# First loads of a two-layer decoder step: order of use, half slabs, and four pieces of the second token half

## The chip, the core and the metric

The kernel runs as one launch on one core of one Trainium2 chip. The core has five engines with a queue of instructions each: TensorE (PE, matrix products), VectorE (DVE), ScalarE (ACT), GpSimd (POOL) and SyncE (SP, which here only issues transfers). Engines meet at semaphores. The metric is the device time of a launch in microseconds; lower is better.

## The reference, cut to what matters

Two layers work on 544 tokens (512 of a prompt, 32 new ones of eight running samples), each token 1024 numbers wide. Layer 0 mixes by a gated recurrence, layer 1 by attention in a sliding window; each is followed by a wide squared-ReLU network, and every residual is normalised. The change touches only the start of layer 0's mixer:

```python
y = jax.nn.gelu(x @ w_y + b_y, approximate=True)
u = x @ w_x + b_x
upad = jnp.concatenate([conv_buf.astype(u.dtype), u], axis=1)
xc = conv_b + sum(conv_w[k] * upad[:, k:k + T] for k in range(CONV_W))
r  = jax.nn.sigmoid(jnp.einsum('btni,nij->btnj', xb, w_ga) + b_ga)    # xb: xc in 8 blocks
gi = jax.nn.sigmoid(jnp.einsum('btni,nij->btnj', xb, w_gi) + b_gi)
a = jnp.exp(-LRU_C * r * jax.nn.softplus(-lam))
h[t] = a[t] * h[t-1] + mult[t] * gi[t] * xc[t]                        # as an associative scan
out = (h * y) @ w_out + b_out
```

## The kernel before, in words

**Layout.** Features lie on the 128 partitions, in eight tiles (k tiles); tokens lie along the free axis, in two halves: half 0 has prompt tokens 0 to 255, half 1 the other 256 and the 32 new ones (288 columns). Every product is made of three: each factor is split into a high part (a float32r copy, made by ACT) and a low part (what the copy lost, made by DVE), and hi·hi, lo·hi and hi·lo are added in PSUM. A split weight needs one ACT and one DVE instruction a slab (128 x 1024), a split pair of token tiles the same.

**Slabs.** SP loads weights in slabs of 512 KB into `stage`, which has four places. ACT's `split` waits for the arrival and writes `w_hi`; DVE's `split` writes `w_lo`, which also frees the place in `stage` (`slab_lo_done`). For pairs of output tiles, `w_x` and `w_y` come as two slabs each, of four k tiles by 256 columns.

**Order of the start.** SP issues, with no wait: tokens of half 0 in four pieces of two k tiles (256 KB each), with the first two slabs of `w_x` among them, the two slabs of `w_y`, then half 1 (1024 KB from `xp_t`, 128 KB from `xs_t` in runs of 32 numbers), and the gate weights once a place is free. ACT issues the vectors of biases and tables (213 KB) behind its first copy. ACT and DVE split the pieces in the order x, slab, x, x, slab, x, slab, slab. PE fills the start with 13 products of constants (`WARM`), then takes the first two `w_x` units k tile by k tile over both units (`group_by_k`), and the two `w_y` units whole, each once both slabs are split.

**The loop over s = 0 to 7** (four pairs of output tiles by two halves) follows. PE takes in step s two units of `w_x`, the gates of step s-1 and two units of `w_y`. ACT copies the `w_x` units to `u`; DVE runs the width-4 convolution into `xc`; ACT and POOL split `xc` (`xc_hi`, `xc_lo`); PE multiplies it by the gates; ACT takes tanh, exp and square root; DVE runs the recurrence (`recur`) and splits the next slabs. Before step 0's convolution, DVE does `derive_in` and `derive_series` (small steps toward a softplus of `lam`) and splits half 1 (`x_split(1)`); behind it comes `derive`. POOL scales the tokens for the residual (`residual0`) once the vectors have landed.

Each engine's order is that of the code. All that the change touches is in `build`: the SP block (lines 483 to 570), the heads of the ACT, DVE and PE blocks, and two inputs of `kernel`.

## Time and profile before

| what | value |
|---|---|
| median of three runs | 1097.09 us (1097.07 to 1097.62) |
| the profiled execution's own time | 1098.72 us |
| its span in the trace | 1096.9 us |
| PE busy | 1076.7 us (98%) |
| DVE, ACT, POOL busy | 802.6, 562.0, 163.7 us |
| granted TensorE clock, mean | 0.996 |

The span runs from the first to the last instruction; 1.82 us of the execution's time lie outside it. A time "at 16.91" is counted from the start of the span. A matmul's shown duration is longer than its step to the next one, because they are pipelined; the step is what a unit costs.

### The profile page before, as it was taken

The numbers are of one execution on the slowest core, as the hardware profiler recorded it, in microseconds if no ns is written. First come the engines' busy times: TensorE is split into PE (matmuls) and PEld (weight loads), VectorE is DVE, ScalarE is ACT, GpSimd is POOL, SyncE is SP. The second block draws the span as 40 slices with busy tenths as digits, with TensorE's granted clock in tenths as the row PEclk, the third lists the DMA queues.
The fourth block names the chain that finished last, engine by engine and source line by source line (L and its number), as shares of the span: only waits on it lengthen the run. The fifth ranks groups of instructions, "written<-read, shape, count | busy, mean of one in ns | idle before, by whom it ended". The sixth has DMA issues, their size and how long they took to land.

```text
span 1096.9 us, 22319 instructions
## 1 busy us (share of the span) xinstructions
PE 1076.7 (98%) x8535; PEld 1054.7 (96%) x8535; DVE 802.6 (73%) x1264; ACT 562.0 (51%) x995; POOL 163.7 (15%) x200
## 2 busy tenths in 40 slices
PE   8999999999999999999999999999999999999996
PEld 7999999999999999999999878999999999999996
DVE  6999899896758568566874574789958668586666
ACT  5999857652433425333666775665533424235233
POOL 2343042000000000011243564300000000000023
PEclk9999999999999999999999999999999999999998
DMA  7323224031413314173041221130423403234202
GB/s 248 115 87 97 74 63 136 19 116 58 136 40 133 117 36 134 44 245 101 20 135 45 61 59 38 48 108 1 154 65 110 134 24 129 72 101 135 77 1 82
DMA packets 63709, 98.66 MB, mean 90 GB/s; under 512 B 4384, under 2 KB 44768, under 8 KB 63616
## 3 DMA queue, kind: packets, MB, share of 16 engines
q1 hardware_dynamic: 62944, 94.81, 27.4%
q0 software_dynamic: 400, 2.21, 0.5%
q8 instruction: 51, 0.84, 0.3%
q10 hardware_dynamic: 288, 0.59, 0.2%
q14 instruction: 26, 0.21, 0.1%
HBM read 95.06 MB, written 3.56 MB: 90 GB/s over the span
## 4 chain that ended last, share of the span: by engine, by line
PE 80%; DVE 10%; ACT 4%; issue 2%; DMA 1%; POOL 1%; SPq 0%; DVEq 0%; ACTq 0%; POOLq 0%
PE bank L1921 10%; PE bank L1922 9%; PE bank L1923 9%; PE bank L2166 8%; PE bank L2168 8%; PE bank L2167 8%; PE bank L2140 6%; PE bank L2142 6%; PE bank L2141 6%; PE bank L1999 2%; PE bank L2001 2%; PE bank L2000 2%; DVE w_lo L1107 2%; PE bank L2275 1%; PE bank L2300 1%
## 5 line engine op out<-in xcount | busy, mean ns | idle before, releaser
L1114 DVE TENSOR_TENSOR w_lo<-stage,w_hi 128x1024 fp32r<-128x1024 f32 x120 | 144.8, 1219 | 56.1 <-ACT w_hi L648 56.1
L648 ACT ACTIVATE w_hi<-stage 128x1024 fp32r<-128x1024 f32 x120 | 124.4, 1054 | 112.5 <-DVE stage L1132 64.7
L1921 PE MATMUL bank<-x_hi,w_hi 128*128 128x288 f32 (+1 forms) x560 | 163.9, 293 | 1.4 <-issue 0.6
L1922 PE MATMUL bank<-m_lo,w_hi 128*128 128x288 f32 (+1 forms) x560 | 162.2, 290 | 0.0
L1922 PE MATMUL bank<-x_lo,w_hi 128*128 128x288 f32 (+1 forms) x560 | 161.7, 289 | 0.0
L1921 PE MATMUL bank<-m_hi,w_hi 128*128 128x288 f32 (+1 forms) x560 | 161.6, 289 | 0.0
L1923 PE MATMUL bank<-m_hi,w_lo 128*128 128x288 f32 (+1 forms) x560 | 161.6, 289 | 0.0
L1923 PE MATMUL bank<-x_hi,w_lo 128*128 128x288 f32 (+1 forms) x560 | 160.9, 287 | 0.0
L2140 PE MATMUL bank<-m_hi,w_hi 128*128 128x288 f32 (+1 forms) x512 | 147.7, 289 | 0.3 <-DVE m_lo L1457 0.3
L2142 PE MATMUL bank<-m_hi,w_lo 128*128 128x288 f32 (+1 forms) x512 | 147.6, 288 | 0.0
L2141 PE MATMUL bank<-m_lo,w_hi 128*128 128x288 f32 (+1 forms) x512 | 147.4, 288 | 0.0
L1469 DVE TENSOR_TENSOR acc<-bank,acc 128x288 f32<-128x288 f32 (+1 forms) x196 | 79.3, 436 | 69.0 <-PE bank L1923 56.2
L869 ACT ACTIVATE h<-bank 128x256 f32<-128x256 f32 (+1 forms) x72 | 28.1, 391 | 177.1 <-PE bank L2168 177.1
L2166 PE MATMUL bank<-s_hi,w_hi 128*128 128x288 f32 (+1 forms) x384 | 112.4, 293 | 0.0
L2167 PE MATMUL bank<-s_lo,w_hi 128*128 128x288 f32 (+1 forms) x384 | 112.1, 292 | 0.0
L2168 PE MATMUL bank<-s_hi,w_lo 128*128 128x288 f32 (+1 forms) x384 | 111.8, 291 | 0.0
L1921 PEld LDWEIGHTS bank<-x_hi,w_hi 128*128 128x128 f32 x560 | 105.2, 188 | 3.3 <-issue 2.4
L1921 PEld LDWEIGHTS bank<-m_hi,w_hi 128*128 128x128 f32 x560 | 105.7, 189 | 0.0
L1922 PEld LDWEIGHTS bank<-m_lo,w_hi 128*128 128x128 f32 x560 | 105.5, 188 | 0.0
L1922 PEld LDWEIGHTS bank<-x_lo,w_hi 128*128 128x128 f32 x560 | 105.3, 188 | 0.1
L1923 PEld LDWEIGHTS bank<-x_hi,w_lo 128*128 128x128 f32 x560 | 105.4, 188 | 0.0
L1923 PEld LDWEIGHTS bank<-m_hi,w_lo 128*128 128x128 f32 x560 | 105.3, 188 | 0.0
(271 smaller groups left out, 2792.4 us busy)
## 6 DMA issues: line engine op xcount, KB each, us to landing
stage<-w_up SPq DMA_DIRECT2D x64, 512.0 KB, 4.4
stage<-w_down SPq DMA_DIRECT2D x64, 512.0 KB, 3.7
stage<-w_qkv SPq DMA_DIRECT2D x10, 512.0 KB, 4.0
stage<-w_x SPq DMA_DIRECT2D x8, 512.0 KB, 5.2
stage<-w_y SPq DMA_DIRECT2D x8, 512.0 KB, 3.6
stage<-w_out SPq DMA_DIRECT2D x8, 512.0 KB, 3.7
stage<-w_o SPq DMA_DIRECT2D x8, 512.0 KB, 3.8
y_t<-acc SPq DMA_DIRECT2D x4, 288.0 KB, 2.4
```

Of the source, the lines that this page charges most:

```text
L648: A(hi, raw, ACT.Copy).then_inc(s_whi, 1)
L1114: vt.tensor_tensor(lo, raw, hi.bitcast(F32), ALU.subtract).then_inc(s_wlo, 1)
L1469: vt.tensor_tensor(a, bank[:, n0 % BANKS, :n], a, ALU.add).then_inc(s_evV, 1)
L1921: mm(out, wh, xh, start=(k == 0), stop=False)
L1922: mm(out, wh, xl, start=False, stop=False)
L1923: ins = mm(out, wl, xh, start=False, stop=(k == last))
L2140: mm(out, wh, xh, start=(k == 0), stop=False)
L2141: mm(out, wh, xl, start=False, stop=False)
L2142: ins = mm(out, wl, xh, start=False, stop=(k == 3))
L2166: mm(out, wh, xh, start=(fresh and k == 0), stop=False, skip_group_check=True)
L2167: mm(out, wh, xl, start=False, stop=False, skip_group_check=True)
L2168: ins = mm(out, wl, xh, start=False, stop=(k == 3), skip_group_check=True)
```

## The change

SP now issues the first loads in the order in which they are used, with the two `w_x` slabs in halves of 256 KB, and with a wait ahead of each from the fifth on: four pieces are out at a time. The two `w_y` slabs wait for the third and fourth token piece, and half 1 waits for the last half of `w_x`. Half 1 is one array now (`x_b`, 288 columns), loaded in four pieces of 288 KB with a semaphore each; half 0 is an array of its own too (`x_a`). ACT and DVE split x, half slab, x, half slab; the issue of the vectors moves behind ACT's third copy. DVE's `derive_series` moves from ahead of `x_split(1)` to behind the convolution and the gates' split. PE takes the `w_y` units of step 0 and the `w_x` units of step 1 by k tile too, and `WARM` is 11.

```diff
@@ -71,12 +71,12 @@
 PROBS = 3
 SPAN = 260
 STAGES = 4
-WARM = 13
+WARM = 11
 SLOTS = 8
 BANKS = 8
 
 
-def build(nc, xp_t, xs_t, vec, w_y, w_x, w_ga, w_gi, w_out, w_qkv, w_o, w_up, w_down,
+def build(nc, x_a, x_b, vec, w_y, w_x, w_ga, w_gi, w_out, w_qkv, w_o, w_up, w_down,
           ck_t, cache_k, cache_v, y_t, small, k_p, v_p, k_s, v_s):
     ctx = ExitStack()
     with ctx:
@@ -180,7 +180,9 @@
 
         s_vec = sem("vec_loaded")
         s_xa = [sem(f"x_half_a_loaded_{k}") for k in range(4)]
-        s_xb = sem("x_half_b_loaded")
+        s_xb = [sem(f"x_half_b_loaded_{k}") for k in range(4)]
+        s_early = [sem(f"first_half_of_slab_{k}_arrived") for k in range(2)]
+        s_halfhi, s_halflo = sem("half_slab_hi_done"), sem("half_slab_lo_done")
         s_arrived = [sem(f"slab_arrived_{i}") for i in range(STAGES)]
         s_whi, s_wlo = sem("slab_hi_done"), sem("slab_lo_done")
         s_unit = sem("unit_done")
@@ -540,23 +542,42 @@
 
             def load_x(k):
                 sp.dma_start(acc[:, 2 * k:2 * k + 2, 0:256],
-                             xp_t[256 * k:256 * k + 256, 0:256].rearrange("(k p) t -> p k t", p=128))\
+                             x_a[256 * k:256 * k + 256, :].rearrange("(k p) t -> p k t", p=128))\
                     .then_inc(s_xa[k], 16)
 
+            def load_half(j, part):
+
+                st = where[j][0]
+                k0 = 4 * j + 2 * part
+                sp.dma_start(stage[:, st, 512 * part:512 * part + 512].rearrange("p (k c) -> p k c", k=2),
+                             xv[:, k0:k0 + 2, 0:256]).then_inc(s_arrived[st] if part else s_early[j], 16)
+
+            def load_xb(k):
+                sp.dma_start(acc[:, 2 * k:2 * k + 2, 256:TOK],
+                             x_b[256 * k:256 * k + 256, :].rearrange("(k p) t -> p k t", p=128))\
+                    .then_inc(s_xb[k], 16)
 
             load_x(0)
-            load(0, xv[:, 0:4, 0:256])
-            for k in (1, 2):
-                load_x(k)
-            load(1, xv[:, 4:8, 0:256])
+            load_half(0, 0)
+            load_x(1)
+            load_half(0, 1)
+            sp.wait_ge(s_xa[0], 16)
+            load_x(2)
+            sp.wait_ge(s_early[0], 16)
+            load_half(1, 0)
+            sp.wait_ge(s_xa[1], 16)
             load_x(3)
-            load_pair(("pair", 0), yv, 0, 2)
+            sp.wait_ge(s_arrived[where[0][0]], 16)
+            load_half(1, 1)
+            sp.wait_ge(s_xa[2], 16)
+            load(2, yv[:, 0:4, 0:256])
+            sp.wait_ge(s_xa[3], 16)
+            load(3, yv[:, 4:8, 0:256])
+            sp.wait_ge(s_arrived[where[1][0]], 16)
+            for k in range(4):
+                load_xb(k)
             for p in range(4):
-                if p == 0:
-                    sp.dma_start(acc[:, :, 256:512],
-                                 xp_t[:, 256:512].rearrange("(k p) t -> p k t", p=128)).then_inc(s_xb, 16)
-                    sp.dma_start(acc[:, :, 512:TOK], xs_t.rearrange("(k p) t -> p k t", p=128)).then_inc(s_xb, 16)
-                else:
+                if p:
                     load_pair(("pair", p), xv, 256 * p)
                     load_pair(("pair", p), yv, 256 * p, 2)
                 j = job_at[("gates", p)][0]
@@ -657,18 +678,24 @@
                 for k in ks:
                     if h == 0:
                         act.wait_ge(s_xa[k], 16)
-                    elif k == 0:
-                        act.wait_ge(s_xb, 32)
+                    else:
+                        act.wait_ge(s_xb[k], 16)
                     A(x_hi[:, 2 * k:2 * k + 2, c0:c0 + n], acc[:, 2 * k:2 * k + 2, c0:c0 + n], ACT.Copy)\
                         .then_inc(s_xhi, 1)
 
-            x_split(0, [0])
+            def split_half(j, part):
+
+                hi, _, raw = split_targets(j)
+                st, at = where[j][0], slice(512 * part, 512 * part + 512)
+                act.wait_ge(s_arrived[st] if part else s_early[j], 16)
+                A(hi[:, at], raw[:, at], ACT.Copy).then_inc(s_whi if part else s_halfhi, 1)
+
             late = VEC["sinks"][0]
-            act.dma_start(vecs[:, 0:late], vec[:, 0:late]).then_inc(s_vec, 16)
-            split([0])
-            x_split(0, [1, 2])
-            split([1])
-            x_split(0, [3])
+            for k in range(4):
+                x_split(0, [k])
+                if k == 2:
+                    act.dma_start(vecs[:, 0:late], vec[:, 0:late]).then_inc(s_vec, 16)
+                split_half(k // 2, k % 2)
             split([2, 3])
             act.wait_ge(s_vec, 16)
             act.dma_start(vecs[:, late:NVEC], vec[:, late:NVEC]).then_inc(s_vec, 16)
@@ -1184,11 +1211,17 @@
             vt.memset(ones[:, :], 1.0 / D).then_inc(s_const, 1)
             vt.memset(tiny[:, 6, :], 0.0).then_inc(s_hsq, 2)
             vt.memset(tiny[:, 7, :], 0.0).then_inc(s_hlo, 2)
-            x_split(0, [0])
-            split([0])
-            x_split(0, [1, 2])
-            split([1])
-            x_split(0, [3])
+            def split_half(j, part):
+
+                hi, lo, raw = split_targets(j)
+                at = slice(512 * part, 512 * part + 512)
+                dve.wait_ge(*((s_whi, j + 1) if part else (s_halfhi, j + 1)))
+                vt.tensor_tensor(lo[:, at], raw[:, at], hi[:, at].bitcast(F32), ALU.subtract)\
+                    .then_inc(s_wlo if part else s_halflo, 1)
+
+            for k in range(4):
+                x_split(0, [k])
+                split_half(k // 2, k % 2)
             split([2, 3])
 
             def derive_in():
@@ -1286,7 +1319,6 @@
             halo(0)
             dve.wait_ge(s_vec, 16)
             derive_in()
-            derive_series()
             for s in range(8):
                 p, h = s // 2, s % 2
                 c0, n = HALF[h]
@@ -1335,6 +1367,7 @@
                     halo(s + 1)
                 if s == 0:
                     split([4])
+                    derive_series()
                     derive()
                     split(next_jobs(0)[:1])
                     dve.wait_ge(s_vec, 32)
@@ -2029,15 +2062,28 @@
                                 for k in range(KT)]
 
                     group_by_k(range(2), 0, pieces0,
-                               lambda k: ((s_xlo, k // 2 + 1), (s_wlo, k // 4 + 1)))
+                               lambda k: ((s_xlo, k // 2 + 1), (s_wlo if k % 4 > 1 else s_halflo, k // 4 + 1)))
+                elif s == 1:
+
+                    def pieces1(t):
+                        return [(*slab(w0, k // 4, 256 * (k % 4) + 128 * t), *act_cols(x_hi, x_lo, k, 1))
+                                for k in range(KT)]
+
+                    group_by_k([mark[("x", 1)] + t for t in range(2)], 1, pieces1, lambda k: ((s_xlo, 5 + k // 2),))
                 else:
-                    if s == 1:
-                        pe.wait_ge(s_xlo, 8)
                     pe.wait_ge(s_wlo, j + 2)
                     for t in range(2):
                         pair_unit(mark[("x", s)] + t, w0, t, h)
                 if s:
                     gates(s - 1)
+                if s == 0:
+
+                    def pieces2(t):
+                        return [(*slab(w0 + 2, k // 4, 256 * (k % 4) + 128 * t), *act_cols(x_hi, x_lo, k, 0))
+                                for k in range(KT)]
+
+                    group_by_k([mark[("y", 0)] + t for t in range(2)], 0, pieces2, lambda k: ((s_wlo, j + 3 + k // 4),))
+                    continue
                 pe.wait_ge(s_wlo, j + 4)
                 for t in range(2):
                     pair_unit(mark[("y", s)] + t, w0 + 2, t, h)
@@ -2486,7 +2532,8 @@
     vec = np.ascontiguousarray(np.concatenate([parts[n] for n in VEC], axis=1))
     kv = NKV * HD
     arrays = {
-        "xp_t": x_prompt[0].T, "xs_t": x_sample.reshape(NS, D).T, "vec": vec,
+        "x_a": x_prompt[0, 0:256].T, "x_b": np.concatenate([x_prompt[0, 256:SEQ], x_sample.reshape(NS, D)]).T,
+        "vec": vec,
         "w_y": lru_w_y[0], "w_x": lru_w_x[0], "w_ga": lru_w_ga[0], "w_gi": lru_w_gi[0], "w_out": lru_w_out[0],
         "w_qkv": swa_w_qkv[0][:, cols], "w_o": swa_w_o[0][q_cols], "w_up": mlp_w_up, "w_down": mlp_w_down,
         "ck_t": cache_swa_k[0].reshape(DEC_B, WIN, kv).transpose(2, 0, 1),
```

SP's queue from its start, with the semaphores that it waits for (`x_half_a_loaded_k`: piece k of half 0 has landed; `slab_arrived_0`: place 0 of `stage`). Before:

```order
L542 DMA acc<-xp_t 128x2x256
L490 DMA stage<-w_x 128x4x256
L542 DMA acc<-xp_t 128x2x256 x2
L490 DMA stage<-w_x 128x4x256
L542 DMA acc<-xp_t 128x2x256
L490 DMA stage<-w_y 128x4x256 x2
L556 DMA acc<-xp_t 128x8x256
L558 DMA acc<-xs_t 128x8x32
L567 DMA stage<-w_ga 128x2x128 [waits slab_lo_done]
```

and in the changed kernel:

```order
L544 DMA acc<-x_a 128x2x256
L552 DMA stage<-w_x 128x2x256
L544 DMA acc<-x_a 128x2x256
L552 DMA stage<-w_x 128x2x256
L544 DMA acc<-x_a 128x2x256 [waits x_half_a_loaded_0]
L552 DMA stage<-w_x 128x2x256 [waits first_half_of_slab_0_arrived]
L544 DMA acc<-x_a 128x2x256 [waits x_half_a_loaded_1]
L552 DMA stage<-w_x 128x2x256 [waits slab_arrived_0]
L492 DMA stage<-w_y 128x4x256 [waits x_half_a_loaded_2]
L492 DMA stage<-w_y 128x4x256 [waits x_half_a_loaded_3]
L556 DMA acc<-x_b 128x2x288 [waits slab_arrived_1]
L556 DMA acc<-x_b 128x2x288 x3
```

Ten issues of half 0, half 1 and the slabs have become fourteen, and the first wait stands ahead of the fifth; the gates' loads stand behind half 1 in both.

DVE's queue from the last two slab splits of the start to the end of `derive_series`; `tiny` holds the steps toward the softplus, `xc_even` is the convolution's result. Before:

```order
L1107 TENSOR_TENSOR w_lo<-stage,w_hi 128x1024 [waits slab_hi_done] x2
L1232 MEMSET u 128x2x3
L1197 TENSOR_SCALAR tiny<-vecs 128x8 [waits vec_loaded]
L1207 TENSOR_SCALAR tiny<-tiny 128x8 [waits softplus_exp]
L1208 RECIPROCAL tiny<-tiny 128x8 [waits vector_order]
L1212 SCALAR_TENSOR_TENSOR tiny<-tiny 128x8 [waits vector_order]
L1181 TENSOR_TENSOR x_lo<-acc,x_hi 128x2x288 [waits x_hi_done,vector_order]
L1308 TENSOR_SCALAR xc_even<-u,vecs 128x256 [waits read_by_scalar]
```

and in the changed kernel, up to the step that follows in `derive`:

```order
L1134 TENSOR_TENSOR w_lo<-stage,w_hi 128x1024 [waits slab_hi_done] x2
L1230 TENSOR_SCALAR tiny<-vecs 128x8 [waits vec_loaded]
L1208 TENSOR_TENSOR x_lo<-acc,x_hi 128x2x288 [waits x_hi_done] x4
L1340 TENSOR_SCALAR xc_even<-u,vecs 128x256 [waits read_by_scalar]
L1134 TENSOR_TENSOR gate_lo<-stage,gate_hi 128x512 [waits slab_hi_done]
L1240 TENSOR_SCALAR tiny<-tiny 128x8 [waits softplus_exp]
L1241 RECIPROCAL tiny<-tiny 128x8 [waits vector_order]
L1245 SCALAR_TENSOR_TENSOR tiny<-tiny 128x8 [waits vector_order]
L1250 SCALAR_TENSOR_TENSOR tiny<-tiny 128x8 [waits vector_order] x5
```

The six steps of `derive_series` have moved from ahead of the four `x_lo` of half 1 to between the gates' split and the five steps of `derive`.

## Rows read from the trace of the kernel before

**Rows 1.** Section 1 of the page: busy time of each engine.

```profile
PE 1076.7 (98%) x8535; PEld 1054.7 (96%) x8535; DVE 802.6 (73%) x1264; ACT 562.0 (51%) x995; POOL 163.7 (15%) x200
```

**Rows 2.** Stretches: length, busy PE, PEld, DVE, ACT, POOL, granted clock, DMA.

```profile
0.00:17.00 17.00, 11.57 (x75) 11.03 (x75) 8.20 (x14) 7.93 (x9) 4.87 (x10) 1.00 0.88 291
17.00:45.00 28.00, 28.00 (x223) 28.00 (x224) 26.87 (x72) 23.89 (x40) 5.64 (x4) 1.00 0.48 150
...
75.00:105.00 30.00, 28.73 (x228) 28.35 (x228) 27.73 (x60) 27.87 (x46) 12.47 (x9) 1.00 0.28 86
```

**Rows 3.** Timeline of PE: start, us, engine, line, tiles [idle before, releaser].

```profile
7.59 0.36 PE L1982 MATMUL bank<-x_hi,w_hi 128*128 128x256 f32 x1 [1.19 <-DVE w_lo L1107]
...
13.53 0.36 PE L1982 MATMUL bank<-x_hi,w_hi 128*128 128x256 f32 x1 [2.86 <-DVE w_lo L1107]
...
16.91 0.39 PE L1921 MATMUL bank<-x_hi,w_hi 128*128 128x256 f32 x1 [0.30 <-DVE w_lo L1107]
...
22.72 0.29 PE L1921 MATMUL bank<-x_hi,w_hi 128*128 128x288 f32 x1
...
42.58 0.30 PE L1921 MATMUL bank<-xc_hi,gate_hi 128*128 128x288 f32 x1
...
97.76 0.37 PE L1921 MATMUL bank<-xc_hi,gate_hi 128*128 128x288 f32 x1 [0.79 <-issue]
...
132.14 0.39 PE L2049 MATMUL bank<-m_hi,w_hi 128*128 128x256 f32 x1 [1.24 <-DVE w_lo L1107]
...
153.75 0.70 PE L1967 MATMUL bank<-sumsq_a,ones 128*128 128x256 f32 x2 [0.25 <-POOL sumsq_a L1819]
```

**Rows 4.** The chain that ended last, 25 to 137 us: start, us, what.

```profile
25.99 1.20 DVE tiny L1217
...
29.12 3.49 DVE w_lo L1107 x3
...
132.11 4.26 DMA stage<-w_out
```

**Rows 5.** Timeline of DVE.

```profile
11.94 1.44 DVE L1107 TENSOR_TENSOR w_lo<-stage,w_hi 128x1024 fp32r<-128x1024 f32 x1 [1.35 <-ACT w_hi L637]
...
15.63 1.23 DVE L1107 TENSOR_TENSOR w_lo<-stage,w_hi 128x1024 fp32r<-128x1024 f32 x1 [0.26 <-ACT w_hi L637]
...
17.49 0.17 DVE L1207 TENSOR_SCALAR tiny<-tiny 128x8 f32<-128x8 f32 x1
...
18.54 0.17 DVE L1212 SCALAR_TENSOR_TENSOR tiny<-tiny 128x8 f32<-128x8 f32 x1
18.86 2.76 DVE L1181 TENSOR_TENSOR x_lo<-acc,x_hi 128x576 fp32r<-128x576 f32 x4 [0.15 <-ACT x_hi L662]
21.55 0.73 DVE L1308 TENSOR_SCALAR xc_even<-u,vecs 128x256 f32<-128x256 f32 x2
...
32.53 0.41 DVE L1308 TENSOR_SCALAR xc_odd<-u,vecs 128x256 f32<-128x256 f32 x1
```

**Rows 6.** Timeline of ACT.

```profile
3.66 0.39 ACTq L667 DMA_DIRECT2D vecs<-vec  x1
...
14.53 1.07 ACT L637 ACTIVATE w_hi<-stage 128x1024 fp32r<-128x1024 f32 x1 [0.42 <-DMA stage<-w_y]
...
18.07 2.40 ACT L662 ACTIVATE x_hi<-acc 128x576 fp32r<-128x576 f32 x4
...
30.33 0.50 ACT L721 ACTIVATE u<-bank,vecs 128x256 f32<-128x256 f32 x1
```

**Rows 7.** Timeline of POOL.

```profile
38.20 1.43 POOL L1801 TENSOR_TENSOR xc_lo<-xc_odd,xc_hi 128x576 fp32r<-128x576 f32 x1 [11.04 <-ACT xc_hi L765]
```

**Rows 8.** DMA of 0 to 20 us in 40 slices; its issues, median us to landing; xp_t alone.

```profile
GB/s 0 0 0 37 63 342 379 387 381 336 318 318 344 350 359 343 339 358 371 383 385 373 356 358 367 385 385 385 318 207 133 241 223 381 308 236 232 258 313 322
...
acc<-xp_t SPq DMA_DIRECT2D x4, 256.0 KB, 6.2
DMA to landing us min/median/max: 2.9/6.8/10.1
```

## The prediction, before the result was known

> **What bounds the kernel now.** Start with the table of busy time [rows 1]: PE is busy for 1076.7 of 1096.9 us, so 20.2 us of it are idle. The table by stretches [rows 2] places that idle time: 17.00 - 11.57 = 5.43 us of it lie in the first 17 us, none from 17 to 45 us, and 1.27 us from 75 to 105 us. By this view alone the start is the place to gain, and whatever PE starts earlier would come off the end.
>
> The timeline of PE [rows 3] names the holes of the start: 1.19 us ahead of the first real product (7.59), 2.86 us at 13.53 for the second slab of w_x, 0.30 us at 16.91 for w_y. The same view holds what speaks against the easy reading. At 97.76, 132.14 and 153.75 PE waits again (0.79, 1.24 and 0.25 us), each time for something of DVE, ACT or POOL. So by then PE has used up its lead, and the others set its pace.
>
> The third view, the chain that ended last, says the same from the other side [rows 4]. Between 25 and 137 us its pieces are not PE's: they are DVE's small steps (25.99), its slab splits (29.12), a load of w_out (132.11) that starts only when a slab has been split. In that stretch DVE and ACT hand the work to each other: DVE is busy for 26.87 of 28 us from 17 to 45, and both for about 27.8 of 30 us from 75 to 105 [rows 2]. PE needs less than they do. The question is therefore not how much earlier PE starts, but how much earlier DVE gets to its first convolution (21.55) and from there to its second (32.53) [rows 5].
>
> How much lead PE has can be read too. It takes the gates of step 1 at 42.58 [rows 3]; POOL had their low part done at 38.20 + 1.43 = 39.63 [rows 7]. The lead is 2.95 us there, and gone at 97.76.
>
> **PE's side: WARM, and units by k tile.** The second w_y slab is split at about 15.3 in the changed kernel (below). PE has done the first half of the two w_y units by then. A w_y pair costs 22.72 - 16.91 = 5.81 us [rows 3], its half 2.9 us, so PE reaches the w_x units of step 1 at about 18.2 instead of 22.72: 4.5 us earlier. That is more than the lead of 2.95 us already there can use: it is added to a lead, and PE waits for the gates of step 1 and at each later place. On the path to the end I count it as 0. The two constant products fewer cost nothing, since PE was idle behind the old thirteen for 1.19 us. Taking half 1 by k tile costs nothing either: the same 48 products in another order.
>
> **The loads.** What DVE waits for last is the second w_y slab: ACT starts its copy at 14.53, behind 0.42 us of waiting for the load [rows 6], and DVE's part ends at 15.63 + 1.23 = 16.86 [rows 5]. In order of use, 3072 KB of tokens and weights and 213 KB of vectors stand up to there, 3.36 MB; with half 1 (1152 KB) it is 4.54 MB. The DMA row [rows 8] shows 318 to 387 GB/s in every slice from 2.5 to 14.5 us; I take 0.36 MB/us from 2.4 us on. Before, 12.1 us of it (4.36 MB) had moved by 14.5: about 1.0 of the 1.18 MB of half 1 had got ahead of the slab. Bounds for the changed kernel: nothing ahead, 2.4 + 9.3 = 11.7; everything ahead, 2.4 + 12.6 = 15.0.
>
> Does holding back starve the queue? The quickest load of 256 KB took 2.9 us from issue to landing [rows 8], and four of 0.262 MB in 2.9 us are 0.36 MB/us, just the plateau. So pieces land some 0.75 us apart from 3.6 on: token pieces at about 3.6, 5.1, 6.6 and 8.1, the last half slab at 9. The second w_y slab is issued at about 8.2 and half 1 right behind it, from 9 to 11, so half 1 still takes its share. I let 0.45 MB of it go ahead: (3.36 + 0.45) / 0.36 = 10.6, landing at 13.0. ACT starts 1.5 us earlier than before. Term: -1.5 us, bounds -2.8 and +0.5.
>
> The Trainium skill, "DMA: Bandwidth & Descriptors", section Bandwidth, speaks against the change: it asks for transfers of 1 MiB or more and gives 64 KB 32% of the peak. By its formula of 2.0 us and bytes over 436 GB/s a piece of 256 KB takes 2.6 us, and four at a time 0.40 MB/us, so even by the page four small pieces do not starve the queue; the row agrees, for its plateau is made of 256 and 512 KB transfers.
>
> **POOL.** Its scaling of the tokens needs the vectors. ACT issued them at 3.66 [rows 6] and now issues them behind the third copy, at about 7.3, so POOL's 4.87 us of the first 17 [rows 2] move some 3 us later, onto the last slab splits. A split beside it took 1.44 us (11.94), one without it 1.23 (15.63) [rows 5]. Term: +0.2 us (bounds 0 and 0.4).
>
> **derive_series.** From 17.49 to 18.54 + 0.17 its six steps take 1.22 us, 1.24 with the step to the next [rows 5]. Ahead of x_split(1) they were free: ACT's first copy of half 1 starts at 18.07 [rows 6], and DVE waits for it until 18.86 in any case, 0.15 us of it idle [rows 5]. The distance from the end of the last slab split to that point, 18.86 - 16.86 = 2.0 us, is ACT's work on the vectors and u and stays. Behind the convolution the six steps stand in a stretch of DVE without a hole, from 21.55 to 32.53, that lies on the chain (25.99 and 29.12 are two of its pieces [rows 4]). Term: +1.24 us (bounds 0, if ACT turned out to be what the second convolution waits for, and 1.24).
>
> **Half 1.** Its four pieces land at about 13.5 to 15.5, and ACT wants the first at 18.07 - 1.5 = 16.6; before, the same. Term: 0. Should a piece be late, the copies wait for it one by one.
>
> **Sum.** -1.5 + 0.2 + 1.24 + 0 = -0.06 us at the convolution of step 1, and everything that follows on the chain moves with it. The profiled execution took 1098.72 us; 1098.66 are forecast for one like it. The median of the runs is 1.63 us below it: 1097.0 us. PE's idle time of the start falls by some 3 us, and later waits of it grow by as much. With the bounds of the forecast's own terms: 1095.7 (loads in strict order) to 1099.0 (-0.06 + 2.0).
>
> **The rivals.**
> - *PE's start passes through* (chance 0.11). For: the 98% and the 5.43 us of the first two views. Against: the waits of PE at 97.76, 132.14 and 153.75. Then the end moves by PE's 4.5 us: 1092.6.
> - *Strict order* (0.16): the second w_y slab lands with nothing of half 1 ahead, at 11.7: -2.8 + 1.44 = -1.4, 1095.7. For: half 1 is issued behind it. Against: half 1 was issued behind it before too, and passed it. The Trainium skill, "DMA: Bandwidth & Descriptors", section Queues, rings and completion order, says that descriptors of one queue are consumed in ring order on each DMA engine; by that rule the slab would have landed at 11.7 before the change already, and the trace, with 14.5, does not agree.
> - *The six steps stay free* (0.08): -1.5 + 0.2 = -1.3, 1095.7; with strict order besides -2.6, 1094.4. Against: ACT's copies of u for the second convolution end at 30.33 + 0.50 = 30.83 [rows 6], 1.7 us before DVE starts on it, so ACT would have to fall back by that much first.
> - *Holding back starves the queue* (0.07), the one on the slow side. The median load of 256 KB took 6.2 us [rows 8], not 2.9. If a held-back piece takes that long with only four out, the second four land at 0.8 + 2 x 6.2 = 13, the second w_y slab, issued at about 12, at 17 or later: 2.5 us later than before, and with 1.44 us of the other terms 1097.1 + 3.9 = 1101.0. It decides from a landing behind 15.3. Against: 6.2 us was the price of a full queue.
>
> **How the numbers follow.** The forecast, 1097.0, has 0.58. What a measurement can tell from no change is 0.2%, 2.2 us. Faster by more: the first rival whole and the double case of the third, 0.11 + 0.04 = 0.15. Slower by more: the last rival, 0.07. Within: 0.78. The range leaves out the first and last rival, and ends at the double case and at the upper bound of the loads: 1094.4 to 1099.0.
>
> **What would show it.** The last w_y split of DVE should end at 15.2 to 15.7 (before 16.86), the first convolution start at about 20.2 (21.55), the second at about 32.4 (32.53). PE's first real product should start at about 5.8, its first half-1 product near 18.2, and PE should wait for the gates by step 1 or 2, at 40 to 60 us, where it did not wait before. The x pieces should land under 4 us after their issue. The forecast is wrong if the second convolution starts more than 1.5 us earlier or later than 32.53, or if it does not and the end moves all the same.

## The result, and the profile after

The changed kernel is slower: 1100.53 us (median of 9 runs, 1099.76 to 1101.06) against 1097.44 (9 runs, 1097.02 to 1098.72). The ratio is 1.0025, with a 95% interval of 1.0015 to 1.0036, so 1.6 to 4.0 us. The forecast was no change, 1097.0 in a range from 1094.4 to 1099.0. The profiled execution took 1100.15 us, its span is 1098.3. TensorE's clock does not explain the loss: with a mean of 0.997 this execution had the highest granted clock of the nine (the others 0.993 to 0.996).

PE has become no busier, and its idle time has only moved. The page's first section and the stretches of after, to set beside [rows 1, 2]:

```profile
PE 1077.0 (98%) x8531; PEld 1054.1 (96%) x8531; DVE 803.0 (73%) x1266; ACT 562.4 (51%) x997; POOL 163.6 (15%) x200
```

```profile
0.00:17.00 17.00, 12.29 (x80) 11.57 (x81) 6.89 (x13) 8.46 (x11) 4.07 (x10) 1.00 0.81 255
17.00:45.00 28.00, 27.08 (x213) 26.54 (x212) 25.69 (x69) 21.41 (x36) 5.62 (x4) 1.00 0.48 158
...
75.00:105.00 30.00, 28.50 (x226) 28.12 (x225) 27.69 (x63) 27.90 (x45) 11.60 (x8) 1.00 0.26 81
```

PE idles 0.72 us less in the first 17 us and 0.92 us more in the next 28. In the same 17 us DVE does less than before (6.89 for 8.20 us), and the DMA moves 255 GB/s where it moved 291. The timeline of PE in after names its waits, as [rows 3] did:

```profile
6.12 0.35 PE L2015 MATMUL bank<-x_hi,w_hi 128*128 128x256 f32 x1 [0.36 <-DVE w_lo L1219]
...
12.68 0.36 PE L2015 MATMUL bank<-x_hi,w_hi 128*128 128x256 f32 x1 [1.30 <-DVE w_lo L1219]
...
21.58 0.29 PE L2015 MATMUL bank<-x_hi,w_hi 128*128 128x288 f32 x1
...
28.56 0.35 PE L1954 MATMUL bank<-xc_hi,gate_hi 128*128 128x256 f32 x1 [0.45 <-POOL xc_lo L1834]
...
44.52 0.35 PE L1954 MATMUL bank<-x_hi,w_hi 128*128 128x256 f32 x1 [0.48 <-ACT z L753]
...
71.10 0.37 PE L1954 MATMUL bank<-xc_hi,gate_hi 128*128 128x288 f32 x1 [0.79 <-issue]
...
134.61 0.38 PE L2095 MATMUL bank<-m_hi,w_hi 128*128 128x256 f32 x1 [1.24 <-DVE w_lo L1134]
```

PE starts real work 1.47 us earlier (6.12 for 7.59) and the first unit of half 1 at 21.58, 1.14 us earlier than 22.72. But it waits already at 28.56 (0.45 us, for POOL's part of the convolution's result), at 44.52 and at 71.10, where before its first such wait was at 97.76, and the wait of 1.24 us that was at 132.14 now ends at 134.61. It has started earlier and reaches that point 2.47 us later.

The two spans differ by 1.4 us only, for the lag does not last to the end. It is still 2.30 us at TensorE's last group of products, 1088.01 in before and 1090.31 after:

```profile
1088.01 1.59 PE L2431 MATMUL bank<-diag,ones 96*128 96x96 f32 x6 [1.68 <-DVE diag L1753]
```

```profile
1090.31 1.29 PE L2477 MATMUL bank<-diag,ones 96*128 96x96 f32 x6 [1.68 <-DVE diag L1786]
```

That group took 0.3 us longer in before, and the other 0.6 us lie behind it, where only the results are scaled and stored. Before's profile is also the slowest of its nine runs (1098.72), which is why the medians differ by 3.1 us and the profiled executions by 1.4.

The timeline of DVE in after shows where the 2.5 us come from, beside [rows 5]:

```profile
16.99 1.23 DVE L1134 TENSOR_TENSOR w_lo<-stage,w_hi 128x1024 fp32r<-128x1024 f32 x1 [1.25 <-ACT w_hi L658]
...
20.15 2.77 DVE L1208 TENSOR_TENSOR x_lo<-acc,x_hi 128x576 fp32r<-128x576 f32 x4 [1.42 <-ACT x_hi L683]
22.83 0.73 DVE L1340 TENSOR_SCALAR xc_even<-u,vecs 128x256 f32<-128x256 f32 x2
...
31.62 3.48 DVE L1134 TENSOR_TENSOR w_lo<-stage,w_hi 128x1024 fp32r<-128x1024 f32 x3
35.03 0.41 DVE L1340 TENSOR_SCALAR xc_odd<-u,vecs 128x256 f32<-128x256 f32 x1
```

The last w_y split ends at 16.99 + 1.23 = 18.22 instead of 16.86: 1.36 us late. The first convolution starts 1.28 us late (22.83 for 21.55), the second 2.50 us late (35.03 for 32.53), since the distance between the two grew from 10.98 to 12.20 us. In front of x_lo DVE now idles 1.42 us, in the place where derive_series used to stand and cost nothing.

Why the split is late stands in the DMA view of after, beside [rows 8] (40 slices of 0 to 20 us; the issues; x_a's landing times):

```profile
GB/s 0 0 0 53 137 383 348 193 236 348 256 303 352 365 174 195 295 227 203 210 271 275 355 303 260 358 323 347 323 328 232 270 357 381 353 355 363 362 417 372
...
acc<-x_a SPq DMA_DIRECT2D x4, 256.0 KB, 4.2
DMA to landing us min/median/max: 2.7/4.2/4.4
```

The plateau of 318 to 387 GB/s is gone: from 3.5 to 12 us the slices lie between 174 and 365. ACT's timeline shows the wait that this makes, beside [rows 6], and SP's how late the last of the w_y slabs goes out:

```profile
10.49 0.63 ACT L683 ACTIVATE x_hi<-acc 128x512 fp32r<-128x512 f32 x1 [1.74 <-DMA acc<-x_a]
...
15.89 1.06 ACT L658 ACTIVATE w_hi<-stage 128x1024 fp32r<-128x1024 f32 x1 [1.41 <-DMA stage<-w_y]
```

```profile
3.44 0.37 SPq L544 DMA_DIRECT2D acc<-x_a  x1
4.62 0.37 SPq L552 DMA_DIRECT2D stage<-w_x  x1
6.07 0.37 SPq L544 DMA_DIRECT2D acc<-x_a  x1
6.79 0.37 SPq L552 DMA_DIRECT2D stage<-w_x  x1
7.46 3.39 SPq L492 DMA_DIRECT2D stage<-w_y  x2
```

SP stands at its waits: the fifth piece goes out at 3.44, the seventh at 6.07, and the second w_y slab waits inside the last row until the token piece issued at 6.07 has landed, at about 10.5.

### The profile page after: what moved, and what is told of

The parts are those of the page before. It is cut to its first block, busy times and chain, and to the rows that moved or that the text cites. A ratio compares the mean times of both kernels' runs of the same rounds, so it can differ in the third digit from the quotient of the medians.

```text
span 1098.3 us, 22317 instructions
## 1 busy us (share of the span) xinstructions
PE 1077.0 (98%) x8531; PEld 1054.1 (96%) x8531; DVE 803.0 (73%) x1266; ACT 562.4 (51%) x997; POOL 163.6 (15%) x200
## 4 chain that ended last, share of the span: by engine, by line
PE 81%; DVE 11%; ACT 4%; issue 2%; DMA 1%; POOL 0%; SPq 0%; DVEq 0%; ACTq 0%
PE bank L1954 10%; PE bank L1955 9%; PE bank L1956 9%; PE bank L2212 8%; PE bank L2214 8%; PE bank L2213 8%; PE bank L2186 6%; PE bank L2188 6%; PE bank L2187 6%; PE bank L2032 2%; PE bank L2033 2%; PE bank L2034 2%; DVE w_lo L1134 2%; PE bank L2321 1%; PE bank L2346 1%
## 5 line engine op out<-in xcount | busy, mean ns | idle before, releaser
L1954 PE MATMUL bank<-x_hi,w_hi 128*128 128x288 f32 (+1 forms) x528 | 154.7, 293 | 2.1 <-ACT z L753 1.4
L1955 PE MATMUL bank<-x_lo,w_hi 128*128 128x288 f32 (+1 forms) x528 | 152.6, 289 | 0.0
L1956 PE MATMUL bank<-x_hi,w_lo 128*128 128x288 f32 (+1 forms) x528 | 151.9, 288 | 0.0
L1954 PEld LDWEIGHTS bank<-x_hi,w_hi 128*128 128x128 f32 x528 | 99.3, 188 | 4.1 <-issue 3.8
L1955 PEld LDWEIGHTS bank<-x_lo,w_hi 128*128 128x128 f32 x528 | 99.4, 188 | 0.1
L1956 PEld LDWEIGHTS bank<-x_hi,w_lo 128*128 128x128 f32 x528 | 99.3, 188 | 0.0
```

What stands on the lines that cost most here:

```text
L1954: mm(out, wh, xh, start=(k == 0), stop=False)
L1955: mm(out, wh, xl, start=False, stop=False)
L1956: ins = mm(out, wl, xh, start=False, stop=(k == last))
```

## The experiments

Twelve kernels in three groups of four, each group beside 33 runs of the kernel before on the same chip (their medians are 1097.46 for a1 to a3 and b1, 1097.05 for c1 to c3 and d1, 1097.90 for a4, a5, d2 and d4). Between groups the ratios compare, not the medians. The theory after the result: two costs add up, the waits that leave too few bytes under way, and derive_series, taken out of a hole in DVE's time and put where there is none. The rival: it is the small pieces or the late vectors, and the moved steps are hidden.

The results, with what the profile of each showed. "Last split" is the end of the last w_y split of DVE, "distance" that from the first to the second convolution:

| kernel | median us | ratio to before (95%) | GB/s 5 to 10 us | last split | distance | 2nd conv. |
|---|---|---|---|---|---|---|
| before | 1097.44 | 1 | 348 | 16.86 | 10.98 | 32.53 |
| changed | 1100.53 | 1.0025 (1.0015 to 1.0036) | 258 | 18.22 | 12.20 | 35.03 |
| a1, no waits | 1098.72 | 1.0012 (1.0003 to 1.0021) | 325 | 16.31 | 12.21 | 33.21 |
| a2, series back | 1099.47 | 1.0016 (1.0007 to 1.0025) | 291 | 17.36 | 10.97 | 33.22 |
| a3, both | 1098.04 | 1.0005 (0.9995 to 1.0014) | 324 | 16.36 | 10.94 | 32.17 |
| b1, series moved | 1099.05 | 1.0015 (1.0006 to 1.0024) | 352 | 15.04 | 12.21 | 31.94 |
| a4, half 1 held | 1098.90 | 1.0007 (0.9998 to 1.0016) | 318 | 16.67 | 12.21 | 33.94 |
| a5, six out | 1098.65 | 1.0010 (1.0001 to 1.0020) | 328 | 16.00 | 12.21 | 33.27 |
| c1, before again | 1097.54 | 1.0003 (0.9993 to 1.0012) | 339 | 16.75 | 10.97 | 32.74 |
| c2, PE's part | 1097.67 | 1.0007 (0.9998 to 1.0016) | 346 | 17.31 | 10.96 | 32.96 |
| c3, before, half 1 held | 1097.48 | 1.0005 (0.9996 to 1.0014) | 349 | 16.62 | 10.95 | 32.77 |
| d1, derive on POOL | 1096.62 | 0.9998 (0.9989 to 1.0007) | 351 | 15.44 | 9.91 | 30.05 |
| d2, and early slab | 1096.57 | 0.9987 (0.9978 to 0.9996) | 338 | 16.96 | 9.16 | 30.96 |
| d4, and PE's part | 1097.73 | 1.0000 (0.9991 to 1.0009) | 331 | 16.70 | 10.15 | 31.48 |

**a1: no waits.** SP's waits between the first loads are gone.

```diff
             load_half(0, 1)
-            sp.wait_ge(s_xa[0], 16)
             load_x(2)
-            sp.wait_ge(s_early[0], 16)
             load_half(1, 0)
-            sp.wait_ge(s_xa[1], 16)
             load_x(3)
...
```

> The changed kernel without SP's waits between the first loads: same order, same halves, same four pieces of half 1, derive_series still moved. Theory (holding back starves the queue, and the moved series costs its 1.24 us): DVE's last w_y split ends within 1 us of the 16.86 of before instead of 18.22, the second convolution starts about 1.2 us behind that of before, and the time is 1.2 us above that of the kernel before, some 1.4 us below the changed kernel. Rival (it is the small pieces, or the late issue of the vectors, not the waits): the last split stays at 18.2 and the time at that of the changed kernel, 2.5 to 3 us above before.

The last split ended at 16.31, 0.55 us before the old 16.86 and 1.91 us before the changed kernel's, and the median is 1.8 us below the changed kernel's and 1.26 above before. The pieces are as small and the vectors as late (issued at 8.37, at 7.47 in the changed kernel), so the rival falls. DVE in a1:

```profile
15.08 1.23 DVE L1127 TENSOR_TENSOR w_lo<-stage,w_hi 128x1024 fp32r<-128x1024 f32 x1 [0.72 <-ACT w_hi L651]
```

**a2: derive_series back.** All loads as changed.

```diff
             derive_in()
+            derive_series()
             for s in range(8):
...
                     split([4])
-                    derive_series()
                     derive()
```

> The changed kernel with derive_series put back ahead of the split of half 1, all else as changed. Theory: the six steps fall into DVE's wait for ACT again, the second convolution starts at 33.8 instead of 35.03, the time is 1.2 us below the changed kernel and 1.4 us above before. Rival (ACT, not DVE, is what the second convolution waits for): no difference to the changed kernel, 2.5 to 3 us above before.

The distance is 10.97 again, and the second convolution starts at 33.22. The time fell by 1.06 us against the changed kernel, as expected (1.2). The second convolution starts 0.6 us sooner than expected because the last split ended at 17.36, although the loads are those of the changed kernel; their rate from 5 to 10 us was 291 GB/s here and 258 there. The start differs that much from one execution to the next.

**a3: both.** The edits of a1 and a2 together:

```diff
             load_half(0, 1)
-            sp.wait_ge(s_xa[0], 16)
             load_x(2)
...
             derive_in()
+            derive_series()
```

> Both edits: no waits between the first loads, and derive_series ahead of the split of half 1. Theory: the two costs add, so that nothing of the loss is left: the time is within 0.7 us of the kernel before, although PE starts its first products and the units of half 1 earlier than before. Rival (small pieces or late vectors): 1.4 us or more above before. Second rival (PE's earlier start passes through once DVE is not late): 2 us or more below before.

0.58 us above before, with an interval that holds 1: nothing of the loss is left that these runs can tell. PE takes its first half-1 product at 19.86 in it, 2.86 us earlier than before, yet the time does not fall below that of before, so the second rival falls too.

**b1: only derive_series moved,** in the kernel before.

```diff
-            derive_series()
             for s in range(8):
...
                     split([4])
+                    derive_series()
                     derive()
```

> The kernel before with one edit: derive_series moved behind the first convolution and the split of the gates. Theory: 1.2 us slower than before, the second convolution at 33.8 instead of 32.53, the first unchanged at 21.55. Rival (the six steps are hidden there too): no difference, within 0.3 us.

1.59 us slower than the runs beside it (ratio 1.0006 to 1.0024), and a distance of 12.21. The absolute places missed: in this profile the first convolution started at 19.73, not 21.55, although its loads are those of before. Identical loads thus end their last split 1.8 us apart from one execution to the next (15.04 and 16.86), which is why the distance and the medians carry the verdict.

**a4: only half 1 held,** the other waits gone.

```diff
-            sp.wait_ge(s_xa[2], 16)
             load(2, yv[:, 0:4, 0:256])
-            sp.wait_ge(s_xa[3], 16)
             load(3, yv[:, 4:8, 0:256])
             sp.wait_ge(s_arrived[where[1][0]], 16)
```

> The changed kernel with one of its waits left, the one ahead of half 1; pieces and w_y slabs are issued at once. Theory: as without any wait, 1.2 us above before (what is left is the cost of the moved derive_series), last w_y split at 15.5 to 16.5. Rival (holding half 1 back lets the w_y slabs through sooner, by up to the 1 MB that used to get ahead): the split ends at 14 to 15 and the time is that of before or below.

As the theory had it, within the noise (last split 16.67, expected up to 16.5). Holding half 1 back brought the w_y slabs nothing.

**a5: six out.** Each wait names a piece two earlier.

```diff
-            sp.wait_ge(s_xa[0], 16)
             load_x(2)
-            sp.wait_ge(s_early[0], 16)
             load_half(1, 0)
-            sp.wait_ge(s_xa[1], 16)
+            sp.wait_ge(s_xa[0], 16)
             load_x(3)
...
```

> The changed kernel with six pieces out at a time instead of four: each wait of SP names the piece that landed two earlier. Theory (few bytes out means a slow queue: four pieces of 0.262 MB landed in 4.3 us each, 0.24 MB/us): six out give about the rate of a full queue; from 5 to 10 us the row of the DMA shows 300 GB/s or more instead of 258, the last w_y split ends near 16.5 instead of 18.22, and the time falls by 1 us or more from that of the changed kernel, to near that without waits (1.3 us above before). Rival (the waits as such, their turn on SP, cost): little change, 2.5 us or more above before.

328 GB/s from 5 to 10 us instead of 258, last split at 16.00, and a ratio of 1.0010 where the changed kernel has 1.0025, some 1.6 us less (the intervals overlap a little, from 1.0015 to 1.0020). There are still waits in SP's queue, so it is not their turn that costs but how little they leave under way. The stretch from 5 to 10 us of the changed kernel, of a5 and of a1:

```profile
5.00:10.00 5.00, 4.12 (x32) 3.78 (x31) 3.39 (x5) 2.78 (x5) 0.00 (x0) 1.00 0.83 258
```

```profile
5.00:10.00 5.00, 3.02 (x24) 2.69 (x23) 3.38 (x5) 3.46 (x6) 0.00 (x0) 1.00 1.00 328
```

```profile
5.00:10.00 5.00, 3.30 (x25) 3.13 (x24) 3.02 (x5) 2.75 (x5) 0.00 (x0) 1.00 0.97 325
```

The last two numbers of each row are the DMA's busy share and its rate: six out are as good as no limit. The two profiles with four out show 258 and 291 GB/s (changed, a2) and last splits at 18.22 and 17.36, the four with more out 318 to 328 and 16.00 to 16.67, so the spread of the start does not cover the difference. PE is the busiest in the slowest of the three, 4.12 of 5 us.

**c1: before again,** without an edit, for a second profile.

> The kernel before, unchanged, for a second profile. Theory: the profile of before that the forecast was read from was a slow draw of the start (1098.72 us, 1.3 above the median), and its last w_y split ended 1 to 2 us later (16.86) than it usually does; here it ends near 15 to 15.5, the second convolution starts near 31, and the time is 1097.4. Rival (the 1.3 us lay elsewhere, at the end of the kernel): the split ends at 16.9 and the second convolution starts at 32.5 again.

This theory fell. The last split ended at 16.75 and the second convolution started at 32.74, as in the first profile, in an execution of 1098.42 us. Both profiles of before are of executions near the top of its runs (1096.02 to 1098.96 in this group), and b1 and d1, with the same first loads, show the other end (15.04, 15.44). What decides between them was not found.

**c2: PE's part alone,** in the kernel before.

```diff
-WARM = 13
+WARM = 11
...
+                    group_by_k([mark[("x", 1)] + t for t in range(2)], 1, pieces1, lambda k: ((s_xlo, 5 + k // 2),))
...
+                    group_by_k([mark[("y", 0)] + t for t in range(2)], 0, pieces2, lambda k: ((s_wlo, j + 3 + k // 4),))
```

> The kernel before with PE's part of the change alone: WARM 11, the w_y units of step 0 and the w_x units of step 1 by k tile; loads, splits and derive_series as before. Theory (PE has a lead here that it can't use): within 0.5 us of before, with the longer lead turned into waits for the gates or banks at 40 to 100 us. Rival (PE's start is worth something): 1 us or more faster. Second rival (both w_y units ending together holds ACT's gelu up): 0.5 us or more slower.

0.62 us more than the runs beside it, with an interval of -0.2 to +1.8 us: no gain, and no loss that these runs can tell. PE's later waits are there as before, and longer (1.18 us at 98.41, and 0.42 at 71.47 where before had none). The profile itself says little on an earlier start: a stretch at the lower clock (below) let PE reach half 1 at 22.35, only 0.37 us earlier than before. a3 and a5, with 19.86 and 19.73, are the better test.

**c3: before with half 1 held** until the second w_x slab has landed.

```diff
                 if p == 0:
+                    sp.wait_ge(s_arrived[where[1][0]], 16)
                     sp.dma_start(acc[:, :, 256:512],
```

> The kernel before with one wait more: SP issues half 1 only when the second w_x slab has landed. Theory (what costs in the changed kernel is the wait per piece; a single wait ahead of half 1 lets the w_y slabs through, and the queue stays full behind it): the last w_y split ends up to 1 us earlier, half 1 lands later but by the time that ACT wants it; the time is between 1 us faster than before and the same. Rival (any gap in the queue costs): half 1 lands behind 17 us, x_split(1) waits for it, and the time is 1 us or more slower.

The same as before within the interval, last split at 16.62 against 16.86 and 16.75. SP issued half 1 at 10.86 instead of 5.15 and the slabs came no sooner than in c1: half 1 had not been what held them up. (The small last loads of half 1 were in time.)

**d1: derive on POOL,** in the kernel before, behind its scaling of half 0.

```diff
                     split([4])
-                    derive()
...
             residual0(0, range(6))
+            pool.wait_ge(s_series, 1)
+            for k in (11, 9, 7, 5, 3):
+                ordered(pt.tensor_scalar(f, f, 1.0, 1.0 / k, ALU.mult, ALU.add))
+                ordered(pt.tensor_tensor(f, f, z2, ALU.mult))
...
```

> The kernel before with the eleven small steps of derive taken off DVE and put on POOL, behind its scaling of half 0 (as seventeen plain steps). Theory (DVE's run between the first and the second convolution sets the end): the second convolution starts 1.0 us earlier after the first (9.9 instead of 10.98 us), where ACT's third copy of a slab (30.3 in the profile of before) is what it then waits for, and the time falls by about 1 us. Rival (the end is set by something else, such as PE): no difference, within 0.4 us.

The distance fell to 9.91, as computed, and DVE now waits 1.77 us for ACT's copy. The time fell by 0.4 us, which the interval (0.9989 to 1.0007) can't tell from nothing. Its eleven runs lie in two groups: the seven with a mean granted clock of 0.996 took 1095.78 to 1096.71 us, the four with 0.993 or 0.994 took 1097.44 to 1098.13. So TensorE's clock may cost over a microsecond where DVE is ahead; no trace of the four shows where.

**d2: and ACT's copy of the next slab earlier,** ahead of the first xc_hi.

```diff
                     split([4])
-                    split(next_jobs(s)[:1])
+                    split(next_jobs(s))
...
                 gelu(s, 1)
-                split(next_jobs(s)[1 + h:])
+                if s:
+                    split(next_jobs(s)[1 + h:])
```

> The kernel before with derive on POOL, as in the run before, and ACT's copy of the next slab moved from behind the first gelu to ahead of the first xc_hi, where ACT sat idle for 2.8 us. Theory: the distance from the first to the second convolution falls from 9.9 to about 8.9 us (10.98 in before), and the time to 1.5 us or more below before, if PE's lead is long enough. Rival (PE's lead is used up: with derive on POOL alone it first waited at 97.97, for 0.47 us): PE holds the time at that of derive on POOL alone, within 0.5 us.

1.33 us below the before of its group, ratio 0.9987 (0.9978 to 0.9996). It is the one kernel of the twelve whose interval lies below 1. The distance is 9.16. The two waits of PE near 100 us are gone; those of the recurrence's end remain:

```profile
124.39 0.35 PE L2057 MATMUL bank<-m_hi,w_hi 128*128 128x256 f32 x1 [0.35 <-ACT z L732]
131.72 0.38 PE L2057 MATMUL bank<-m_hi,w_hi 128*128 128x256 f32 x1 [1.26 <-DVE w_lo L1109]
```

**d4: and PE's part of the change,** d2 with the edit of c2.

> The same with PE's part of the change on top (WARM 11, w_y units of step 0 and w_x units of step 1 by k tile). Theory (PE's earlier start has a value only where DVE and ACT are ahead of it): up to 1 us below the same kernel without it. Rival (DVE and ACT set the end even here): no difference, within 0.4 us.

The theory fell: 1.2 us more than d2 in the medians, the intervals just overlapping. The profile shows one way in which this can happen: taken by k tile, both w_x units of step 1 end together, and ACT waits for the first. ACT and then DVE in d4:

```profile
28.71 0.29 ACT L720 ACTIVATE us<-bank,vecs 128x32 f32<-128x32 f32 x1 [1.08 <-PE bank L1992]
```

```profile
30.34 1.23 DVE L1109 TENSOR_TENSOR w_lo<-stage,w_hi 128x1024 fp32r<-128x1024 f32 x1 [2.29 <-ACT w_hi L638]
```

DVE waits 2.29 us for ACT where d2 had 1.10 and the distance is back at 10.15. PE took its first half-1 product at 22.48, before d2's 23.54, and in d2 ACT found the first unit ready. Taken whole, the first unit would have been done 24 products later, at about 25.7 (an estimate: 0.133 us a product), and ACT asked at 28.71 - 1.08 = 27.63. PE was late all the same, by a stretch at the lower clock (below), so the 1.08 us need both. Whether they are the 1.2 us of the medians is not shown: the edit also has WARM 11, and five of its eleven runs have a mean clock of 0.992 or 0.994, in d2 two.

## Why the prediction was wrong

**The loads: this step failed.** The forecast put the term at -1.5 us; the trace has +1.36. The sentence that failed is the one on whether holding back starves the queue. It took the quickest landing of 256 KB, 2.9 us [rows 8], as the time that each of four pieces would need, so that four out gave just the plateau of 0.36 MB/us. The 2.9 us is the first piece's, issued into an empty queue. With four out the pieces of x_a took 4.2 us in the median: 4 x 0.262 / 4.2 = 0.25 MB/us, and 258 GB/s is what the changed kernel shows from 5 to 10 us. The second w_y slab landed at 15.87, behind the 15.3 that the rival had named, where the forecast had 13.0. a5 and a1 settle it: 328 and 325 with six out or all. By the medians the waits cost 1.8 us (changed against a1) or 1.4 (a2 against a3).

The formula that the prediction took from the Trainium skill, "DMA: Bandwidth & Descriptors", stands there in the section Anatomy of one DMA, not in Bandwidth, as a fit for single transfers issued from GpSimd, where here SP issues. The 2.6 us of a piece are an estimate from it: the first piece agrees (2.7), those with four out do not (4.2 in the median), and the measurement decides. The row that the prediction called in agreement had all loads issued at once, so it could not show what four out bring.

The rival on the slow side named this mechanism. Its 6.2 us a piece was too much, and so were its 1101.0 and its price for the loads (+2.5). It had a chance of 0.07, because the 6.2 us were taken for the price of a full queue alone; the truth lay between 2.9 and 6.2.

**What orders would bring.** The forecast also had 0.45 MB of half 1 ahead of the last slab where 1.0 MB had been, a gain of 1.5 us without a stall. a1 and a4 have no stall and end the last split at 16.31 and 16.67, c3 at 16.62: inside the spread of the seven profiles that have the first loads of before (before, b1, c1, c2, d1, d2, d4: 15.04 to 17.31). No gain from the order is visible in DVE's last split. In the changed order the rate also dips without waits: a1's slices from 3.5 to 6 us read 223, 176, 229, 303 and 191 GB/s, against 387, 381, 336, 318 and 318 [rows 8]. Whether that is the halves or the new arrays was not tried.

**derive_series: right.** 1.24 us forecast, 12.20 - 10.98 = 1.22 in the trace; in runs 1.06 us (changed against a2), 0.68 (a1 against a3) and 1.59 (b1, against the runs beside it). It was free in front of x_split(1) and is not behind the convolution.

**POOL: not seen.** The +0.2 did not come. POOL's six steps ran from 12.69 to 16.56, and the split at 16.99 took 1.23 us. The one at 14.52 ran beside POOL and took 1.23 too, as two such splits did in b1 (12.32 and 13.81), so the 1.44 us of the prediction's row were not POOL's doing in general. **Half 1: 0, right.** ACT's first copy of it waited for its own work, not for the load.

**PE's side: right in its term, off in its size.** PE's half-1 product came 1.14 us early, not the 4.5 of the forecast, since w_y was late. But the step's point held where PE was 2.9 and 3.0 us early (a3, a5): an earlier PE adds to a lead that it can't use. In the changed kernel the waits behind the start begin at 28.56, not at 97.76. The rival that PE's start passes through is refuted by a3 as well.

**The chain: right.** The second convolution set the end: the first product of a later stage that waits on DVE (214.29 in before, 216.61 after) follows it by 181.8 and 181.6 us, and by 181.5 to 182.8 in all fourteen profiles, while the second convolution itself starts anywhere from 30.05 to 35.03. What the forecast called its test, a shift of over 1.5 us of the second convolution, came out at 2.50, and the end moved with it: 2.32 us at that product, 3.1 in the medians (1.4 in the two profiled executions, for the reason given with the result). The sum with the measured terms is +1.36 + 1.22 = 2.6.

## What to carry to other kernels

Holding transfers back needs enough bytes out for the rate wanted times the landing time under load; the landing of the first transfer in an empty queue is too short for that sum. Here, by an estimate from a5, 0.33 MB/us times 4.6 us ask for 1.5 MB out; the change left 1.05 MB. Small steps that look free to move should be priced at both places: in a hole of their engine they cost nothing, and in its unbroken run all of their time. Before making the busiest engine start earlier, look at what it waits for later: if the others set its pace, what it gains at the start comes back as a wait, and the time is to be had where they hand work to each other (d2: the steps of derive and one copy of ACT moved, 1.3 us).

## What was not expected of the hardware

The same first loads end at different times: 15.04 to 17.31 us for the last split over the seven profiles named above, more than most of the edits are worth.

The granted clock of TensorE fell in the start in five of the fourteen profiles: c1, c2, c3, d2 and d4. c1, the same program as before, waited 2.49 us up to 13.29 and ran at half, 1.2 instead of 2.4 GHz, from 14 to past 17; d4 waited 3.30 us up to 8.47 and ran at half from there to 14. The waits ahead of it in c2, c3 and d2 were 2.32, 2.15 and 2.02 us. Before waited 2.86 us and a2 2.89 us, and both kept their clock. Rows of c1 and of d4 (as [rows 2]):

```profile
13.00:14.00 1.00, 0.71 (x6) 0.74 (x7) 0.75 (x2) 1.00 (x1) 1.00 (x2) 0.99 1.10 383
14.00:15.00 1.00, 1.00 (x7) 1.00 (x6) 0.96 (x1) 0.58 (x2) 1.00 (x2) 0.50 1.12 288
```

```profile
12.00:13.00 1.00, 1.00 (x7) 1.00 (x6) 1.00 (x2) 0.39 (x2) 1.00 (x1) 0.50 1.09 363
...
15.00:16.00 1.00, 1.00 (x11) 1.00 (x10) 0.94 (x2) 0.45 (x1) 0.00 (x0) 1.00 1.04 253
```

The counts of a row take in every product that touches its slice, so they don't give the speed. The timeline does: at half clock a product of 256 columns follows the last after 0.21 us, at full clock after 0.12. Two pairs of c1:

```profile
14.36 0.41 PE L1983 MATMUL bank<-x_lo,w_hi 128*128 128x256 f32 x1
14.58 0.41 PE L1984 MATMUL bank<-x_hi,w_lo 128*128 128x256 f32 x1
...
18.08 0.28 PE L1921 MATMUL bank<-x_hi,w_hi 128*128 128x256 f32 x1
18.20 0.28 PE L1922 MATMUL bank<-x_lo,w_hi 128*128 128x256 f32 x1
```

By the same step a3's products at 6.17 and 6.38 ran at half clock, where its row shows 1.00; so the 1.00 of the first microseconds is not to be relied on. In c1 the stretch at half clock used up some of PE's lead, but not all that mattered: the distance stayed at 10.97, and PE still had to wait at 98.21 (0.58 us).
